# A 32-slot lowest-ranked expert, gathered results and down blocks in row pairs in a two-layer hybrid backbone with eight experts

## The reference, cut to what matters

```python
def swiglu(h, w_gate, w_up, w_down):
    return (jax.nn.silu(h @ w_gate) * (h @ w_up)) @ w_down

def moe_swiglu(h, w_router, b_router, w_gate, w_up, w_down):
    logits = (h @ w_router).astype(jnp.float32) + b_router.astype(jnp.float32)
    top_v, top_i = lax.top_k(logits, TOP_K)
    top_w = jax.nn.softmax(top_v, axis=-1)
    gates = jnp.sum(jax.nn.one_hot(top_i, N_EXPERTS, dtype=jnp.float32) * top_w[..., None], axis=-2)
    ...
    for e in range(N_EXPERTS):
        out = out + gates[..., e:e + 1] * swiglu(h, w_gate[e], w_up[e], w_down[e])
    return out
...
    # the last step of the last layer
    h_lat = h_lat + mod_lat[5] * rmsnorm(ffn(f_lat), g_post_ffn[l])
```

## Time and profile before

| | before |
|---|---|
| median of 3 runs | 1733.86 us (1733.58 to 1742.61) |
| the profiled execution | 1735.59 us, its span 1733.9 us |
| mean granted TensorE clock | 0.982 |
| busy in the span: TensorE, its weight loads | 1654.6 us (95%), 903.6 us (52%) |
| DVE, ACT, GpSimd | 651.4, 354.8, 73.3 us |
| read from HBM | 389.36 MB, 225 GB/s over the span |

### The profile page before, as it was taken

One profiled execution on the slowest core, in us unless ns is written; L12 is line 12 of the kernel. 1 busy time (PEld: TensorE's weight loads), 2 busy tenths in 40 slices (PEclk: granted clock), 3 DMA queues, 4 the chain that ended last, 5 costly groups with the idle time before them and its releaser, 6 DMA issues.

```text
span 1733.9 us, 24936 instructions
## 1 busy us (share of the span) xinstructions
PE 1654.6 (95%) x10477; PEld 903.6 (52%) x10477; DVE 651.4 (38%) x1505; ACT 354.8 (20%) x760; POOL 73.3 (4%) x147
## 2 busy tenths in 40 slices
PE   6999999889999999998997989999999999999997
PEld 3655454368888864444775764334334433333332
DVE  4987972565454511409589371000100010001002
ACT  4334452221110100004555332000000000000002
POOL 2210100000000030000101000000000000000000
PEclk9999999989999999999999979999999999999999
DMA  8513743452333242226144239999999999999995
GB/s 312 157 14 111 251 106 130 149 134 61 93 98 97 67 84 74 67 101 239 56 139 117 57 129 403 409 405 407 409 409 389 394 405 409 404 407 409 409 405 227
DMA packets 195023, 396.29 MB, mean 229 GB/s; under 512 B 34371, under 2 KB 104619, under 8 KB 188762
## 3 DMA queue, kind: packets, MB, share of 16 engines
q1 hardware_dynamic: 189536, 391.23, 61.9%
q0 software_dynamic: 4112, 3.34, 1.3%
q10 hardware_dynamic: 1258, 0.07, 0.0%
HBM read 389.36 MB, written 1.05 MB: 225 GB/s over the span
## 4 chain that ended last, share of the span: by engine, by line
PE 88%; DVE 4%; DMA 3%; ACT 2%; SPq 1%; issue 1%; ACTq 0%; DVEq 0%
PE ps L1025 85%; PE ps L1028 3%; SPq L548 1%; DMA norms<-in_moe_w_down_dram 1%; DMA ring<-in_w_in_dram 1%; DVE norms L1905 1%; DMA ring<-in_moe_w_down_dram 1%; DVE hT L1927 1%; DVE aT L1913 0%; DVE work L1922 0%; ACT dg L710 0%; DVE aT L1922 0%; ACT work L701 0%; ACT work L702 0%; ACT work L817 0%
## 5 line engine op out<-in xcount | busy, mean ns | idle before, releaser
L1025 PE MATMUL ps<-ring,work 128*32 128x256 f32 (+5 forms) x3192 | 422.2, 504 | 3.6 <-DMA ring<-in_moe_w_down_dram 1.5
L1025 PEld LDWEIGHTS ps<-ring,work 128*32 128x32 f32 (+2 forms) x3192 | 157.7, 120 | 256.5 <-issue 227.0
L1025 PE MATMUL ps<-work 128*64 128x64 f32 (+11 forms) x2320 | 236.9, 327 | 9.8 <-DVE work L2189 5.1
L1025 PE MATMUL ps<-aT,ring 128*128 128x256 f32 (+1 forms) x800 | 236.9, 446 | 2.9 <-ACT aT L774 2.2
L1025 PE MATMUL ps<-work,ring 128*128 128x512 f32 (+1 forms) x656 | 237.0, 514 | 1.3 <-DVE work L2221 1.3
L2379 DVE TENSOR_TENSOR work<-work,ps 128x512 f32<-128x512 f32 (+4 forms) x27 | 19.5, 731 | 541.5 <-PE ps L1025 541.5
L1025 PEld LDWEIGHTS ps<-work 128*64 128x64 f32 (+5 forms) x2320 | 157.3, 150 | 80.3 <-issue 65.1
L1025 PEld LDWEIGHTS ps<-aT,ring 128*128 128x128 f32 x800 | 153.0, 193 | 73.7 <-issue 55.3
L1025 PE MATMUL ps<-aT,work 128*128 128x256 f32 (+6 forms) x1116 | 186.7, 468 | 0.3 <-DMA aT<-in_moe_w_down_dram 0.3
L1025 PEld LDWEIGHTS ps<-work,ring 128*128 128x128 f32 x656 | 124.5, 190 | 106.5 <-issue 98.5
L1025 PEld LDWEIGHTS ps<-aT,work 128*32 128x32 f32 (+2 forms) x1116 | 105.4, 143 | 68.0 <-issue 52.2
(11 more groups left out here) (354 smaller groups left out, 1297.7 us busy)
## 6 DMA issues: line engine op xcount, KB each, us to landing
ring<-in_moe_w_up_dram SPq DMA_DIRECT2D x57, 1024.0 KB, 14.3
ring<-in_moe_w_down_dram SPq DMA_DIRECT2D x49, 1024.0 KB, 15.1
ring<-in_w_ada_dram SPq DMA_DIRECT2D x23, 2048.0 KB
ring<-in_moe_w_gate_dram SPq DMA_DIRECT2D x37, 1024.0 KB, 13.9
ring<-in_moe_w_up_dram SPq DMA_DIRECT2D x28, 768.0 KB, 15.2
aT<-in_moe_w_gate_dram SPq DMA_DIRECT2D x17, 1024.0 KB, 14.2
aT<-in_moe_w_down_dram SPq DMA_DIRECT2D x17, 1024.0 KB, 16.9
ring<-in_moe_w_gate_dram SPq DMA_DIRECT2D x18, 768.0 KB, 15.1
```

The lines of the kernel that those rows point to most:

```text
L1025: return pe.matmul(o, lhs, rhs, start=start, stop=stop)
```

## The change

- Slots: the lowest rank (7, `TINY`) has 32 slots instead of 64, 640 in all. Its products with gate, up and down use 32 columns of the array each, four side by side, 256 weight columns each. The capacities `cap` follow.
- Order: the pairs are (1,4), (0,6), (2,5) and (3,7). In the last one the two ranks don't alternate: the three chunks of rank 3 come first, then the three of rank 7.
- Results: the upper 32 rows of the three mid experts (`yX`, 96 rows) are spread together in the product behind rank 3 (`spread_alone`, in the up blocks of item 21), so a spread of the first three pairs has one product for each quarter. `SgB`, `yL`, `yB` and the six extra gate transposes go; ACT copies the tiny expert's gate rows four times into `GtT`.
- End: `carry` brings the sum in `hT` into PSUM by eight products with the identity, in the up blocks of items 22 and 23. After the last down block ACT and DVE copy one 64x256 piece each (`yT`), and `spread_end` adds eight products of 32 rows by 256 columns onto that sum, in banks 5, 6, 0 and 1. The norm then reads PSUM; ACT and DVE take turns on it.
- Row pairs: the down blocks of full-width, heavy and tiny items are loaded as `(p k)`, partition p holding rows 2p and 2p + 1, which are neighbours in HBM (70 of 88 down blocks); `turn_h` takes every second column of `hs` for them (`turned_cols`).

```diff
-        SLOTS = [P] * NW + [HP + TP] * NM_ + [HP] * NH
+        TINY = NE - 1
+        SLOTS = [P] * NW + [HP + TP] * NM_ + [HP] * NM_ + [TP]
...
         yH = view(9472, [D], "n")
-        yL = view(10496, [512], "n")
-        Gt = view(11008, [NE + NM_, S], "r t")
+        yX = view(10496, [D], "n")
+        yT = view(5120, [256], "n")
+        Gt = view(11520, [NE, S], "r t")
+        GtT = view(13568, [S], "t")
...
-        yB = sg[:, 0, :]
+        yD = sg[:].rearrange("p b t -> p (b t)")
...
-        PAIRS = [1, 0, *range(2, NH)]
-        items = [(r, c) for p in PAIRS for c in range(NC) for r in (p, NH + p)]
+        PAIRS = [(1, 4), (0, 6), (2, 5), (3, TINY)]
+        LAST = PAIRS[-1][0]
+        items = [(r, c) for pair in PAIRS[:-1] for c in range(NC) for r in pair]
+        items += [(r, c) for r in PAIRS[-1] for c in range(NC)]
         NI = len(items)
+        ALONE = NI - NC
+        SPREADS = 4 * NH + 4
+        END = (5, 6, 0, 1)
...
+        def tiny(i):
+            return items[i][0] == TINY
...
+            if tiny(i):
+                return 2, 0, TP * (w // 256), 0
...
+        def row_pairs(i):
+
+            return width(i) == 1024 or heavy(i) or tiny(i)
+
+        def turned_cols(i, c0, t):
+
+            if row_pairs(i):
+                return slice(c0 + 2 * P * (t // 2) + t % 2, c0 + 2 * P * (t // 2) + 2 * P, 2)
+            return slice(c0 + P * t, c0 + P * t + P)
...
+            if tiny(i):
+                return [(slice(0, TP * (w // 256)), 0, 0, 256)]
...
-        MOVED = KC + 5
+        MOVED = KC + 4
+
+        def end_sum(q):
+
+            tt, g = divmod(q, 2)
+            return ps[:, END[2 * g]:END[2 * g] + 2, S * tt:S * tt + S]
...
-                def load(n, i, src):
+                def load(n, i, src, paired=False):
...
-                    sp.dma_start(wblock(n)[:, :, 0:src.shape[2]], src.rearrange("e (k p) n -> p (e k) n", p=P))\
+                    order = "e (p k) n -> p (e k) n" if paired else "e (k p) n -> p (e k) n"
+                    sp.dma_start(wblock(n)[:, :, 0:src.shape[2]], src.rearrange(order, p=P))\
...
-                    load(n, i, moe_down[0, bass.ds(expert[r], 1), f0 + 256 * d:f0 + 256 * d + 256, :])
+                    load(n, i, moe_down[0, bass.ds(expert[r], 1), f0 + 256 * d:f0 + 256 * d + 256, :], row_pairs(i))
...
                     act.activation(xg[:, k, :], ps[:, b:b + 2, :].rearrange("p b n -> p (b n)")[:, 0:NSLOTS], ACT.Copy)\
                         .then_inc(sem("moved"), 1)
                 for i in range(4):
-                    act.wait_ge(sem("gates_turned"), 5 * ph + i + 1)
+                    act.wait_ge(sem("gates_turned"), 4 * ph + i + 1)
                     act.activation(Gt[:, 4 * (i // 2):4 * (i // 2) + 4, P * (i % 2):P * (i % 2) + P],
                                    ps[:, 4 + i, :].rearrange("p (r s) -> p r s", r=4), ACT.Copy).then_inc(sem("moved"), 1)
-                act.wait_ge(sem("gates_turned"), 5 * ph + 5)
-                act.activation(Gt[:, NE:NE + NM_, :].rearrange("p r (t s) -> p t r s", t=2),
-                               ps[:, 4:6, 0:P * NM_].rearrange("p t (r s) -> p t r s", r=NM_), ACT.Copy).then_inc(sem("moved"), 1)
+                act.wait_ge(sem("moved"), MOVED * ph + MOVED)
+                for q in range(4):
+                    act.activation(GtT[TP * q:TP * q + TP], Gt[P - TP:P, NH, :], ACT.Copy)
 
                 def copy_turned(i):
...
+                def copy_alone():
+
+                    act.wait_ge(sem("block_used"), b0 + down_end[ALONE - 1])
+                    act.wait_ge(sem("spread"), SPREADS * ph + 4 * (NH - 1))
+                    for g in range(2):
+                        for q in (2 * g, 2 * g + 1):
+                            act.activation(yX[TP * (LAST - NW):TP * (LAST - NW) + TP, 256 * q:256 * q + 256],
+                                           ps[TP * q:TP * q + TP, 6, 0:256], ACT.Copy)
+                        act.activation(yD[HP * g:HP * g + HP, 512 * g:512 * g + 512], ps[HP * g:HP * g + HP, 5, :], ACT.Copy)\
                             .then_inc(sem(f"y_ready{g}"), 1)
...
+                    if i == ALONE:
+                        copy_alone()
                 copy_turned(NI - 1)
-                copy_y(NH - 1)
+                act.activation(root_tick[:], eps_t[:], ACT.Sqrt)
+                act.wait_ge(sem("block_used"), b0 + n_blocks)
+                act.activation(yT[0:HP], ps[0:HP, 7, 0:256], ACT.Copy).then_inc(sem("y_ready0"), 1)
...
-                act.wait_ge(sem("summed"), a + 1)
-                act.activation(quarter_of(hs[:, tt, 0:512]), result(a), ACT.Square,
+                act.wait_ge(sem("spread"), SPREADS)
+                act.wait_ge(sem("y_scaled7"), a)
+                act.activation(quarter_of(hs[:, tt, 512:D]), end_sum(b), ACT.Square,
+                               scale=D ** -0.5, accum_out=ssq[:, b:b + 1]).then_inc(sem("squared"), 1)
+                act.wait_ge(sem("squared"), 3 * tt + 1)
+                act.activation(ssq_e[:, tt:tt + 1], ssq[:, b:b + 1], ACT.Identity, bias=eps_t[:, 0:1]).then_inc(sem("squared"), 1)
+                act.wait_ge(sem("y_scaled7"), a + 1)
+                act.activation(quarter_of(hs[:, tt, 0:512]), end_sum(a), ACT.Square,
                                scale=D ** -0.5, accum_out=ssq[:, a:a + 1]).then_inc(sem("squared"), 1)
-                act.wait_ge(sem("squared"), 3 * tt + 1)
-                act.activation(ssq_e[:, tt:tt + 1], ssq[:, a:a + 1], ACT.Identity, bias=eps_t[:, 0:1]).then_inc(sem("squared"), 1)
-                act.wait_ge(sem("summed"), b + 1)
-                act.activation(quarter_of(hs[:, tt, 512:D]), result(b), ACT.Square,
-                               scale=D ** -0.5, accum_out=ssq[:, b:b + 1]).then_inc(sem("squared"), 1)
                 act.wait_ge(sem("squared"), 3 * tt + 3)
-                act.activation(rms[:, tt:tt + 1], ssq[:, b:b + 1], ACT.Sqrt, bias=ssq_e[:, tt:tt + 1]).then_inc(sem("rms_ready"), 1)
+                act.activation(rms[:, tt:tt + 1], ssq[:, a:a + 1], ACT.Sqrt, bias=ssq_e[:, tt:tt + 1]).then_inc(sem("rms_ready"), 1)
...
                         for j in range(4):
                             last = turn(ps[:, 4 + i, P * j:P * j + P], Sg[:, i % 2, 4 * (i // 2) + j, :])
                         last.then_inc(sem("gates_turned"), 1)
-                    pe.wait_ge(sem("moved"), MOVED * ph + KC + 2)
-                    for i in range(2):
-                        for j in range(NM_):
-                            last = turn(ps[:, 4 + i, P * j:P * j + P], SgB[:, i, j, :])
-                    last.then_inc(sem("gates_turned"), 1)
 
                 def turn_h(i, j):
...
-                        last = turn(ps[:, 4, P * t:P * t + rows], hs[0:rows, i % 2, c0 + P * t:c0 + P * t + P], rows)
+                        last = turn(ps[:, 4, P * t:P * t + rows], hs[0:rows, i % 2, turned_cols(i, c0, t)], rows)
                     last.then_inc(sem("h_turned"), 1)
...
+                            elif tiny(i):
+                                lhs = xg[:, k, SLOT0[r]:SLOT0[r + 1]]
+                                for g in range(w // 256):
+                                    last = mm(ps[TP * g:TP * g + TP, bank, 0:256], lhs,
+                                              b[:, j, 256 * g:256 * g + 256], k == 0, k == KC - 1)
...
+                            if tiny(i):
+                                for g in range(4):
+                                    last = mm(ps[TP * g:TP * g + TP, 7, 0:256], hTs[:, i % 2, j, TP * d:TP * d + TP],
+                                              b[:, j, 256 * g:256 * g + 256], first, end)
+                                continue
...
-                                    at_ = HP * (1 - g if r >= NH + NW else g)
+                                    at_ = HP * (1 - g)
...
-                def spread(p, q, bank):
+                def spread(p, q):
 
                     tt, g = q // 2, q % 2
                     if q < 2:
                         pe.wait_ge(sem(f"y_ready{q}"), 2 * (p0 + p + 1))
-                    if bank == 4 and q:
-                        pe.wait_ge(sem("spread_added"), 4 * (p0 + p) + q)
-                    o = ps[:, bank, :]
-                    tok, half = slice(P * tt, P * tt + P), slice(HP * g, HP * g + HP)
-                    r = PAIRS[p]
-                    if r < NW:
-                        mm(o, Gt[:, r, tok], yH[:, 512 * g:512 * g + 512], True, False)
-                        mm(o, Gt[half, NH + r, tok], yL[half, :], False, True).then_inc(sem("spread"), 1)
-                        return
-                    mm(o, Gt[:, NH * g + r, tok], yH[:, 512 * g:512 * g + 512], True, False)
-                    mm(o, Gt[half, NE + r - NW, tok], yB[half, :], False, True).then_inc(sem("spread"), 1)
+                    if q:
+                        pe.wait_ge(sem("spread_added"), SPREADS * ph + 4 * p + q)
+                    o = ps[:, 4, :]
+                    r = PAIRS[p][0]
```

(88 more changed lines are left out.)

75 lines of the change are left out of this document (34 added, 41 removed).

## The result

The changed kernel takes 1721.64 us (median of 6 runs, 1721.19 to 1722.57) where the kernel before takes 1733.73 us beside it (6 runs, 1732.79 to 1742.61): ratio 0.992, 95% interval 0.990 to 0.994. That is 12.1 us less; 14.2 were forecast, to 1719.7, and the range holds the time. (Beside the later experiments the kernel before had medians of 1734.7 to 1735.3 us, so the gain may be 1 us more.) Its profiled execution lasted 1721.49 us with a span of 1719.8.

The account below looks back on a forecast made before the run. The prediction took TensorE as the bound from 1030 to about 1352 us, then the DMA stream to 1714.9, then 19.0 us of end. Landing -9.7 and end -4.5 made -14.2: 1719.7 us from 1733.86, range 1714.5 to 1727.5.

Parts of the forecast that it names:

- Step 1: Ahead of the experts: shorter second gather part and six fewer gate transposes, -1.5 us on TensorE's path.
- Step 2: Spreads of the first three pairs: one product for two, 4.4 us less each, only the first pair's ahead of 1352 us.
- step 5: Turns of hidden rows from every second column: no change taken; upper bound a doubling, +1.0 us per full-width item.
- Step 3: 70 down blocks read in 8 KB pieces: 2.56 to 2.47 us each, -6.7 us over the stream.
- Step 4: DMA stream: the 3.2 us starvation about gone, plus the faster blocks; last landing moves by -9.7 us.
- rival C: Every second column costs double in the turns of hidden rows: 1724.7 us; chance 0.12.
- Step 6: Last pair: three mid items in a row cause no new starvation; TensorE then waits for DMA in the 32-slot items.
- Steps 7 and 8: From last landing to end: 19.0 to 13.4 us (-5.6), plus 1.2 for a lower clock; -4.5 us rounded.
- Rival B: Row pairs in the down loads bring only 0 to 2 us: 1726.2, or 1724 with the 2 us; chance 0.14.
- D: The end does not shorten: products in line at the lower clock eat the 4.5 us, 1724 to 1725; chance 0.13.
- E: Slower: row pairs make the DMA stream slower, from 1743 us; chance 0.03.
- F: Lowest expert has more than 32 tokens, so the second pass runs: another 680 us, about 2400; chance 0.02.

Follow-up runs that it names:

- twice_first: Changed kernel with the product of each spread of the first pair issued a second, redundant time; 1725.6 us.
- twice_later: Changed kernel with the products of the second and third pair's spreads issued twice; 1722.1 us.
- after_no_pairs: Changed kernel without row pairs: all down blocks read as two 4 KB pieces, hidden rows turned from neighbouring columns; 1724.5 us.
- before_pairs: Kernel before with only the row pairs added, with their load order and every-second-column turns; 1734.6 us, ratio 0.9993.
- all_8k: Changed kernel with all 1 MB blocks in 8 KB pieces, full-width gate and up blocks read from the down matrix (wrong sum); 1716.9 us.
- all_4k: Changed kernel with every 1 MB block in 4 KB pieces, full-width gate and up blocks read from the down matrix (wrong sum); 1725.4 us.
- end_one_group: Changed kernel with all eight products of the end taking their 32 rows from the same row group (wrong output); 1727.4 us.
- before_heavy_third: Kernel before with the heavy pair third instead of second, nothing else changed; 1740.9 us, ratio 1.004.

## Why the prediction was right, by its steps

Its reading, TensorE to about 1352 us and the stream from there, is what twice_first and twice_later show: the same kind of work costs its whole length at 1215 us and nothing after 1350.

Step 1 (-1.5 us): from the same start, the item after the gate transposes begins at 1074.07 instead of 1075.41, -1.3; in after_no_pairs, without the new turns, it is -1.5. The gate transposes are 16 records, 1.97 us for 2.71.

Step 2 (-4.4 for the first pair): 36.20 became 31.40 us in the chain, -4.8. Steps 1 and 2 gave 5.9 together, measured are 6.1; 5.3 are there at 1383, because step 5 takes the rest.

Step 3 (row pairs, -6.7): the mechanism is right, the size a little high. A block wins 0.073 us, which makes 70 x 0.073 = 5.1; measured are 3.9 to 5.3 in the landings and 2.8 by the medians. By the packet overhead that the Trainium skill states (DMA: Bandwidth & Descriptors, Why small descriptors are slow) it would be an estimated 1%; measured are 2.9% from 4 to 8 KB pieces. The forecast's own slip was to put a line through rows of 14 to 30 us, where the stream ran free at 425; in the expert stage 8 KB pieces run at 421.

Step 4 (landing -9.7): -7.8. Two terms were over-sized: the blocks' gain by about 1.6, and the starvation, of which 0.9 us is left. "About gone" was written for a sum of 3.2 + 2.8 - 5.9 = 0.1; the turns of step 5, which it puts at nothing, hold TensorE back by 0.9 us there. That this is the remainder is an inference; no run takes the turns alone away. The step's own rule, that a faster stream enlarges the starvation by what it wins ahead of the heavy pair's end, is borne out by before_pairs (3.2 became 6.2 us) and all_8k. What it did not ask is how much TensorE has to spare behind that point: 2.9 us in the kernel before, so there the pairs alone bring next to nothing, and 15.6 us in the last 100 of the changed kernel, so here they count. The forecast's reading of the earlier trace rows is loose in its words (three of the 18 slices are at 410 to 420 GB/s, above its 402), while its sum of 3.2 us is right.

Step 5 (no price for every second column): not quite. The four turns of an item take 0.75 us with it and 0.66 without, in the timeline of the first item. The chain has the sum: from the first item behind the gather to the end of the heavy pair TensorE needs 312.86 us in the kernel before and 313.76 in before_pairs, where nothing else of its work differs; another 0.16 is lost ahead of it. First the timeline's lines of the changed kernel and of the kernel before, then the chains of before and of before_pairs:

```profile
1071.02 0.75 PE L1076 MATMUL ps<-ident,work 128*128 128x128 f32 x4
1072.52 0.66 PE L1028 MATMUL ps<-ident,work 128*128 128x128 f32 x4
```

```profile
1075.41 26.36 PE ps L1025 x240
...
1388.27 31.77 PE ps L1025 x240
```

```profile
1074.55 26.36 PE ps L1036 x240
...
1388.31 31.77 PE ps L1036 x240
```

That is 1.06 us from the gather on, for nine row-pair items: about a tenth of a microsecond each, where rival C feared 1.0. The changed kernel shows the same 0.9 between 6.1 and 5.3 us above. At most this much reaches the end, so rival C is excluded, though its mechanism is there at a tenth of its size.

Step 6 (three mid items without new starvation): the stream stays at 409 to 410 GB/s in 1500 to 1700 us, and TensorE waits for DMA in the last 60 us. With 8 KB pieces throughout it does not starve there either (416 in 1600 to 1690). With the heavy pair third it does, in this very place (384 GB/s in 1580 to 1640 us). Both fit the step's reading that the three mid items live on the lead won in the pair ahead of them.

Steps 7 and 8 (end -4.5): -6.3, to 12.6 us, below the 13 to 15 that it named as its sign. The products were 1.11 us (1.3), the copies 0.44 and 0.14 (0.5), the spread 1.24 (2.0), the rest 9.7 (9.6). What was over-sized is the spread, by 0.8, and the clock, by 1.2: the window of 1706 to 1712 us has it at 1.00. In other executions of the same end it was lower, and the products and the spread were up to 1.92 and 2.18 us (twice_first). The windows of the changed kernel:

```profile
1700.00:1706.00 6.00, 4.37 (x50) 2.20 (x50) 0.42 (x1) 1.82 (x3) 0.00 (x0) 1.00 0.60 250
1706.00:1712.00 6.00, 2.22 (x32) 1.19 (x32) 1.98 (x4) 2.17 (x8) 0.00 (x0) 1.00 0.05 18
```

So two errors of nearly 2 us, of opposite sign, made a sum of -14.1 in the profile for the forecast's -14.2: the mechanisms were right, that the sum fits to 0.1 us is luck. The 1.9 us by which the median misses come from the last line of the sum. It took the change off the median, but the profiled execution of before (1735.59 us) is itself 1.9 us above that kernel's median (1733.7), while the changed kernel's (1721.49) lies on its own; with starts of the gather that differ by 3 us from one execution to another, this is the accuracy that one profile has.

Rival B (pairs bring 0 to 2 us), C and D (the end does not shorten) are all excluded by a run: B by all_8k beside all_4k, C by the chain of before_pairs, and D by end_one_group, which shows what D would have been (18.7 us of end for 12.6). E, a slower stream, does not occur: outside the dip no window of 100 us or more with paired blocks is slower than its unpaired one. F, a second pass of some 680 us, is excluded by the time itself.

## What to carry to other kernels

When two resources are both full, ask of each saving on which side of the change-over it lies: here a spread saved before 1350 us brought its whole length, the same one later nothing, and faster transfers alone next to nothing, because the other resource had 3 us to spare; together they brought 2 to 5 us more than the sum of both. So read for each side how much slack the other one leaves. A transfer's lead can be stored in buffers and a compute engine's cannot, so the heaviest compute belongs where the buffers are full and not behind light work "to save up" for it. And compare stages from a common start in each profile: medians of a kernel whose early part wanders by 3 us hide effects of that size.

## What the runs showed of the hardware that was not expected

- The last 6 us of the stream run at little more than half rate. The DMA view of 1690 to 1710 us of the changed kernel (busy tenths and rate of 40 slices of 0.5 us) shows it from 1700.5 us on; the kernel before has the same tail from 1709.5. The last blocks land later by some 2.5 us than bytes over the full rate would say. The forecast moved measured landings, so it cancelled.

```profile
DMA  9999999999999999999997755646455430000000
GB/s 418 387 369 406 418 408 410 428 430 395 399 399 410 432 389 446 375 397 434 426 377 311 295 229 246 262 197 262 197 213 213 197 147 0 0 0 0 0 16 0
```

- The clock granted in the end differs between executions: 1.00 for 1706 to 1712 us in the changed kernel, 0.50 in end_one_group, with the same program up to the last spread, worth up to 1.8 us in the changed kernel's end and 6.0 us in before_heavy_third's.
- Eight fp32 products of 32 rows in four row groups and four banks take 1.24 us at the full clock and 2.18 at 0.50; in one group 7.17 at 0.50.
- Transposes whose stationary operand takes every second column cost 0.09 us more for four of 128x128 (0.75 against 0.66 us).
